# A two-layer hybrid decoder step on one core: new orders at six seams, and the four low parts of one operand sum in each MLP opening on GpSimd

## The reference, cut to what matters

```python
xp = xp + attention(rmsnorm(xp, norm_mix[0])) @ attn_w_out       # layer 0
xp = xp + sq_relu_mlp(rmsnorm(xp, norm_mlp[0]), mlp_w1[0], mlp_w2[0])
xp = xp + rec_mixer(rmsnorm(xp, norm_mix[1]), ...)               # layer 1
xp = xp + sq_relu_mlp(rmsnorm(xp, norm_mlp[1]), mlp_w1[1], mlp_w2[1])

def sq_relu_mlp(xn, w1, w2):
    h = jax.nn.relu(jnp.einsum('btd,df->btf', xn, w1))
    return jnp.einsum('btf,fd->btd', h * h, w2)
```

## Time and profile before

| | |
|---|---|
| median of 3 runs | 2592.11 us (2590.67 to 2595.39) |
| the profiled execution's own time | 2595.46 us |
| its span, first to last instruction | 2593.6 us |
| TensorE busy | 2454.6 us, 95% |
| VectorE busy | 1806.3 us, 70% |
| ScalarE busy | 1256.1 us, 48% |
| GpSimd busy | 1332.7 us, 51% |
| mean granted TensorE clock | 0.969 of full |
| chain that ended last | PE 58%, DVE 6%, issue 2%, ACT 2%, POOL 2%, DMA 1% |

### The profile page before, as it was taken

How to read it: one execution, slowest core, us unless ns; L and a number is a source line. 1 busy time by engine, 2 the same in 40 slices (tenths; PEclk the granted TensorE clock), 3 DMA queues, 4 the chain that set the end, 5 groups by cost and what they waited for, 6 DMA issues and landing times.

```text
span 2593.6 us, 46703 instructions
## 1 busy us (share of the span) xinstructions
PE 2454.6 (95%) x17442; PEld 2274.9 (88%) x17442; DVE 1806.3 (70%) x2986; ACT 1256.1 (48%) x2318; POOL 1332.7 (51%) x904
## 2 busy tenths in 40 slices
PE   7999999989878999998999989998989999899999
PEld 6667788856668999998999988997989999899999
DVE  5367766436559777776877776566587777687777
ACT  5348884866534455553332343435245555433322
POOL 4114550027334466666777762323336666587775
...
DMA packets 171513, 360.56 MB, mean 139 GB/s; under 512 B 29621, under 2 KB 69685, under 8 KB 171013
## 3 DMA queue, kind: packets, MB, share of 16 engines
...
## 4 chain that ended last, share of the span: by engine, by line
PE 58%; DVE 6%; issue 2%; ACT 2%; POOL 2%; DMA 1%; SPq 0%; ACTq 0%; DVEq 0%; POOLq 0%
PE d_ps L3311 24%; PE d_ps L3265 23%; PE d_ps L2411 10%; DMA hidden_parts<-plain_tail 1%; PE d_ps L3662 1%; DVE plain_rows L2795 1%; DVE row_parts L2783 1%; POOL plain_tail L2438 1%; POOL row_parts L2957 1%; DVE row_parts L2814 1%; DVE x_t L2678 0%; ACT plain_tail L2432 0%; DVE row_parts L3790 0%; POOL weight_parts L2946 0%; DVE plain_rows L2790 0%
## 5 line engine op out<-in xcount | busy, mean ns | idle before, releaser
L3265 PE MATMUL d_ps<-row_parts,weight_parts 128*128 128x272 f32 x5376 | 686.4, 291 | 19.3 <-DVE row_parts L2814 12.0
L3265 PEld LDWEIGHTS d_ps<-row_parts,weight_parts 128*128 128x128 f32 x5376 | 684.3, 191 | 21.0 <-issue 21.0
L3311 PE MATMUL d_ps<-row_parts,weight_parts 128*128 128x272 f32 x5376 | 680.5, 289 | 22.3 <-POOL row_parts L2957 17.3
L3311 PEld LDWEIGHTS d_ps<-row_parts,weight_parts 128*128 128x128 f32 x5376 | 678.7, 190 | 24.1 <-issue 20.1
L3430 DVE TENSOR_TENSOR x_t<-x_t,d_ps 128x544 f32<-128x544 f32 (+1 forms) x512 | 392.9, 785 | 117.0 <-PE d_ps L3311 114.3
L2411 PE MATMUL d_ps<-row_parts,weight_parts 128*128 128x364 f32 (+1 forms) x1944 | 342.9, 337 | 32.8 <-DVE row_parts L2626 12.1
L2411 PEld LDWEIGHTS d_ps<-row_parts,weight_parts 128*128 128x128 f32 x1944 | 333.7, 193 | 39.1 <-issue 23.3
L2876 POOL TENSOR_TENSOR weight_parts<-unit_raw,weight_parts 128x512 fp32r<-128x512 f32 x124 | 162.0, 1307 | 241.3 <-ACT weight_parts L2872 241.3
L2942 ACT ACTIVATE weight_parts<-unit_raw 128x512 fp32r<-128x512 f32 x128 | 80.2, 627 | 383.2 <-DVE unit_raw L2922 364.9
L2946 POOL TENSOR_TENSOR weight_parts<-unit_raw,weight_parts 128x512 fp32r<-128x512 f32 x128 | 174.4, 1362 | 127.8 <-ACT weight_parts L2942 124.8
L2957 POOL TENSOR_TENSOR row_parts<-row_parts 128x1088 fp32r<-128x1088 f32 x80 | 204.4, 2572 | 29.5 <-ACT row_parts L2952 29.5
...
## 6 DMA issues: line engine op xcount, KB each, us to landing
...
```

Source lines behind the costliest of these rows:

```text
L3265: last = nc.tensor.matmul(out[:, c, :], m.ring(i, e)[:, P * kp:P * (kp + 1)], m.side(i, f, kp)[:, HC * c:HC * (c + 1)], start=(i in (0, 1, ...
L3311: last = nc.tensor.matmul(out[:, c, :], m.part_slot(g, i, e)[:, P * q:P * (q + 1)], m.hidden_row(b, i, f)[:, at:at + HC], start=(i in (0, ...
```

## The change

Six seams get new orders. Nothing is computed otherwise.

1. **Sample attention to output projection.** Rows 0 and 1 of `mixed_t` are loaded by SyncE while the sample attention still runs, into a new tile `early_rows` that lies over a part of SBUF that is free by then. The other four are issued by SyncE instead of ScalarE, and the last eight of twelve small window-row loads (`own_rows`) come behind them. ScalarE makes the high part of unit 1, and VectorE, not GpSimd, the low parts of units 0 and 1, in turn with those of rows 0 and 1.
2. **Output projection to MLP 0.** GpSimd makes `weight_low` 0 and 1 in step n = 3 instead of 4 and 2 in step 4 instead of 5; ScalarE makes `weight_high` 0 to 2 in step 3 and 3 and 4 in step 6. In the last step VectorE no longer makes parts of `fourth` and of operand 4 ahead of the addition of unit 7. In the MLP `mean(0)` now comes first, then operand 5; the reciprocal is cut into three pieces (544, 480 and 64 columns), all behind `mean(1)`; the ones product of the sample tokens stands behind product 6 instead of 5. All four `low_of` of operand 6 move from VectorE to GpSimd.
3. **MLP 0 up to down.** The loads of hidden operands 2 to 6 move from ScalarE to SyncE, behind the stores of pair 14; ScalarE makes the high part of hidden operand 0 ahead of the last `copy`.
4. **MLP 0 down to the recurrent block.** Squares, sums and the split of the first two recurrent units move up into the last three steps; VectorE takes the last two sums from GpSimd.
5. **Recurrent output projection to MLP 1** as 2, and 6. **MLP 1 up to down** as 3.

The diff, cut to its core:

```diff
@@ stage_sample, sync
-            for n, g in enumerate((1, 0)):
-                for x in range(NA + DB // 4 * n, NA + DB // 4 * (n + 1)):
-                    sp.wait_ge(o_out[x % NO], 16 * (x // NO + 1))
-                own.load_b(sp, g)
+            for k in range(EARLY_ROWS):
+                sp.dma_start(smp.early_rows[:, k, :], mixed[k][:, TS:TS + SEQ]).then_inc(early[f"op_mixed_in{k}"], 16)
+            for x in range(NA, NA + DB // 4):
+                sp.wait_ge(o_out[x % NO], 16 * (x // NO + 1))
+            own.load_b(sp, 1)
@@ stage_out_projection, sync
-            own.load_b(sp, 2)
+            for k in range(EARLY_ROWS, NK):
+                sp.dma_start(d.out_row(k, 1)[:, rows].bitcast(F32), mixed[k][:, rows]).then_inc(mixed_in[k], 16)
+            for g in (0, 2):
+                own.load_b(sp, g)
@@ gpsimd
-            d.split_low(pool, HOME_OUT, 0, 0)
-            d.split_low(pool, HOME_OUT, 1, 1)
-                for i in {4: (0, 1), 5: (2,), 6: (3, 4), 7: (5, 6)}.get(n, ()):
+                for i in {3: (0, 1), 4: (2,), 6: (3, 4), 7: (5, 6)}.get(n, ()):
@@ scalar
+                if k == 0:
+                    act.wait_ge(d.w_in[1], 16)
+                    act.wait_ge(d.w_high, 1)
+                    nc.scalar.activation(d.unit(HOME_OUT, 1, 0), d.raw[:, 1, :], ACT.Copy).then_inc(d.w_high, 1)
@@ vector, start and last step
-            weights_high(0)
-            weights_high(1)
-            for k in range(NK - 1):
+            dve.wait_ge(d.w_in[0], 16)
+            nc.vector.tensor_copy(d.unit(HOME_OUT, 0, 0), d.raw[:, 0, :]).then_inc(d.w_high, 1)
+            weights_low(0)
+            low_of(0)
+            weights_low(1)
+            for k in range(1, NK - 1):
                 low_of(k)
...
-                if n == KD - 1:
-                    dve.wait_ge(last_read, 1)
-                    mlp.fourth(dve, KP - 2)
-                    mlp.low_of(dve, 3, KP - 2)
-                    dve.wait_ge(last_read, 3)
-                    for kp in range(KP - 1):
-                        mlp.low_of_row(dve, 4, kp)
...
+                    if n == KD - 1:
+                        dve.wait_ge(last_read, 1)
+                        mlp.fourth(dve, KP - 2)
+                        mlp.low_of(dve, 3, KP - 2)
+                        d.sum_up(dve, n, 0)
...
-            mlp.low_of_row(dve, 4, KP - 1)
+            dve.wait_ge(last_read, 3)
             for kp in range(KP):
-                mlp.low_of_row(dve, 5, kp)
+                mlp.low_of_row(dve, 4, kp)
@@ stage_mlp, sync
+            if n == UPS - 1:
+                for i in range(2, NPROD):
+                    sp.wait_ge(m.up_made, NPROD * n + (0, 0, 2, 2, 3, 3, 4)[i])
+                    load_hidden(sp, 0, i)
             early_stores(n)
@@ gpsimd
+        for kp in range(KP):
+            m.low_of(pool, 6, kp)
@@ tensor
-                if n == 0 and i == 5:
+                if n == 0 and i == NPROD - 1:
                     pe.wait_ge(m.gathered, 3)
@@ vector
+        mean(0)
+        for kp in range(KP):
+            m.low_of_row(dve, 5, kp)
+        for x in range(2):
+            gather(0, x)
+        for x in range(2):
+            m.weigh(dve, 1, x)
+        gather(0, 2)
+        for x in range(2, 4):
+            m.weigh(dve, 1, x)
+        gather(0, 3)
+        mean(1)
+        invert(0)
+        scale(0, 0)
+        for t in (1, 2):
+            invert(t)
+        for x in (1, 2):
+            scale(0, x)
@@ scalar, down
+            if g == DOWNS - 1 and y is None:
+                unit_high(0)
...
-                if k > 1:
-                    next_squares(k - 2)
+                next_squares(k - 1)
```

156 lines of the change are left out of this document (69 added, 87 removed).

## The result

| | before | after |
|---|---|---|
| median of 4 runs each | 2593.75 us (2590.67 to 2603.64) | 2567.38 us (2565.48 to 2572.54) |
| the profiled execution's own time | 2595.46 us | 2566.12 us |
| its span | 2593.6 us | 2564.3 us |
| TensorE busy | 2454.6 us | 2442.5 us |
| mean granted TensorE clock | 0.969 | 0.978 |

The ratio is 0.9895, with a 95% interval of 0.9864 to 0.9926: faster, by 26.4 us of median and 29.3 us of profiled span. The total came out; the parts did not all do so.

The account below looks back on a forecast made before the run. TensorE, busy 95% of the span, bounds the kernel, so only its idle stretches can be won. Terms -3.5 + 1.9 - 1.9 + 1.0 - 15 - 9 = -26.5 us gave 2566 us; range 2551 to 2582.

Parts of the forecast that it names:

- Seam 1: Sample attention to output projection: TensorE starts 3.9 us earlier, less 0.4 for the early load; -3.5 us, bounds -4 and -1.
- The out-projection step: Output projection, steps 3 to 6: weight lows on GpSimd block VectorE, delaying unit 6; +1.9 us, bounds 0 and +3.5 (half clock).
- The openings: Output projections' ends into MLP 0 and MLP 1 (seams 2, 5): -1.9 and +1.0 us, bounds -7 and +4 each.
- The walk: First opening, each engine followed in the new order at estimated instruction prices: 16.7 us lost instead of 18.6.
- My first rival: Openings: operand 6's lows finish during products 2 to 4, waits for products 4 and 5 vanish; 2556 us, chance 0.25.
- My 1.8 us: Openings: price of a VectorE instruction with two SBUF inputs while GpSimd works back to back, instead of 0.7 us.
- Seams 3 and 6: End of up to down, both MLPs: earlier copy and hidden low parts; -7.5 us each, -15 together, bounds -2 and -9 each.
- the step on the third relu: Seams 3 and 6: operand 3's high part follows the third relu, ends at 1181; GpSimd is through at 1193.2.
- my 12.4 us for GpSimd: Seams 3 and 6: GpSimd's back-to-back work from hidden operand 3 on, before product 6 of down can start.
- My second rival: Seams 3 and 6: hidden loads come late, gaining 2.5 instead of 7.5 us at each; 2576 us, chance 0.17.
- Seam 4: MLP 0 down to recurrent block: the eighth square's chain moves 8.3 to 9.4 us earlier; -9 us, bounds -5 and -11.
- The rival that ended slower: Openings: many short waits keep the granted clock at half, costing more per up matmul; some 2633 us, chance 0.03.

## Why the prediction was right, and where its steps failed

**Seam 1 held, by its time alone.** The first matmul came at 741.37; I said 740 to 741. The part gave 2.8 of 3.5 us (2.2 to 3.0 in eleven of the twelve other runs). No run took the early rows or the low parts on VectorE back, so which of them gave it is argued, not shown.

**The out-projection step was right in mechanism and short by the clock.** The wait for unit 6 was 1.76 us (I had 1.9), and undoing the two lows removed it. What I kept for the upper bound only, half clock, came with it: 108 matmuls took 19.79 us instead of 18.3. The term is +3.1, and it came so in nine of the ten runs that kept that order.

**The openings were mis-sized, mostly by the clock.** The walk gave waits of 2, 3.5 and 5.5 us, 11.0 in all, and a loss of 16.7, which leaves 5.7 for a late operand 5 and for half clock, not told apart. The trace has waits of 0.85, 2.15, 5.52 and 1.63, 10.2 with operand 5, and 1.5 of clock in MLP 0 (2.7 in MLP 1). So the last wait was exact, and the chain behind it (`mean(1)`, three reciprocals, scalings, `gather`) is the right one. The failed steps: "operand 5's four low parts ... up to 4 x 1.8 = 7.2 us" took 4.99, since GpSimd was through with operand 6 at 841.4 and with one weight low at 843.1, and then rested; and the half clock that the 5.7 us took in came only behind the longest wait. My first rival, "the openings win as well" by 5 us each, had the size for MLP 0 (4.1 us better than forecast) and about half of it for MLP 1 (2.7). Its reason, waits for products 4 and 5 vanishing, didn't happen.

**Whose work blocks whom was priced about right, and it costs.** With operand 6 back on VectorE the trace shows 2.86 instead of 4.99 us for the same four instructions. (My 1.8 us is not the mean of the row that I named, 6.67 us for five, which is 1.33; the changed kernel's 7.15 us for four, 1.79 each, bears it out.) The page "SBUF — State Buffer" (Who interferes with whom) of the Trainium skill has VectorE's second SBUF input and GpSimd's reads share a port; that agrees with these two numbers. The page "GPSIMD Engine Reference" (4.1 Engine selection) of the Trainium skill keeps an elementwise add on VectorE; by it I had estimated 2.6 us less per opening, and 1.0 was measured up to product 2 of the second pair, in both.

**Seams 3 and 6: the step on the third relu failed.** I wrote that operand 3's high part would be through at 1181, 0.9 us behind the end of up, and GpSimd at 1193.2. It ended at 1176.51, 2.6 us behind the end of up, because the copy still stood for a store (5.74 us), which I had ruled out with "Now the store precedes the loads". It precedes five operands, not the loads of operands 0 and 1, and behind it DMA is full (360 to 417 GB/s from 1160 on). Nor would an earlier copy have done: with the copy 3.3 us earlier operand 3's own load held its high part at the same place, a wait that my walk put at nothing. From that high part on my 12.4 us for GpSimd was near, 12.9. So 5.6 and 4.7 us instead of 7.5. My second rival, late hidden loads, holds a share: never as TensorE's releaser, but with operand 3 loaded first and its high part ahead of the relu the seams were 2.6 and 2.9 us shorter.

**Seam 4 held:** -9.9 against -9, and undoing it cost 11.0. TensorE waited 1.43 us for `convolve` where I had 2, and 63 matmuls took 10.73 instead of 12.26 us.

**The rival that ended slower, a clock that stays at half,** didn't come: at 834.5 us it was at 1.00, and the mean rose to 0.978. The total fell into my range because errors of both signs nearly cancelled: -6.8 for the openings, +4.7 for seams 3 and 6, +1.9 for seam 1 and the projection, -0.9 for seam 4, and -1.7 that I had no term for. Of the last, 1.2 us is the recurrent stretch, where the same 2.91 us wait was followed by 63 matmuls in 12.30 instead of 13.52 us: clock, and luck. That the total is right to within 3 us is luck too. What is not luck is most of its size: seams 3, 4 and 6 gave 20 of the 29 us, and undoing them took that back.
